# Transposing x unscaled, scaling the forget products by token, and forming the normalised input alongside

## The reference

```python
def rms_norm(x, gain):
    y = x * lax.rsqrt(jnp.mean(x * x, axis=-1, keepdims=True) + NORM_EPS)
    return y * gain

h = rms_norm(x, pre_norm)
z = einsum('btd,dn->btn', h, w_in)          # 12848 columns, split by use:
(a_q, a_kc, a_vc, a_ks, a_vs, a_kw, a_vw, a_gate, a_silu,
 b_v, b_silu, c_q, c_f, c_i, c_silu, merge_logits) = split(z)

# the gated recurrence ("HGRN2") reads the forget columns c_f first
f = lb + (1 - lb) * sigmoid(c_f)            # per token and channel
logf, k = log(f), 1 - f                     # then cumulative sums of logf by chunk
...                                         # attention, pooling, gates
out = einsum('btd,de->bte', merged, w_out)
x = x + rms_norm(out, post_norm)
```

## Time and profile before

| | us |
|---|---|
| median of 3 runs (lowest, highest) | 480.6 (480.55, 480.81) |
| the profiled execution | 480.7 |
| its span, first to last instruction | 478.8 |

### The profile page before, as it was taken

The page is one execution under the profiler, slowest core; times in us unless marked ns, Lnnn a source line. Parts: engine busy times, 40 slices in busy tenths (PEclk is TensorE's granted clock), DMA queues, the critical chain, the costliest instruction groups (busy, mean ns, idle before and its releaser), DMA issues.

```text
span 478.8 us, 9549 instructions
## 1 busy us (share of the span) xinstructions
PE 471.5 (98%) x3884; PEld 459.6 (96%) x3884; DVE 347.8 (73%) x611; ACT 278.0 (58%) x418; POOL 170.0 (35%) x157
## 2 busy tenths in 40 slices
...
GB/s 296 324 165 182 225 134 130 141 54 175 177 144 122 142 266 210 99 174 179 88 252 104 166 97 89 90 175 89 176 96 169 177 152 192 185 244 241 175 1 90
DMA packets 75994, 76.47 MB, mean 160 GB/s; under 512 B 5745, under 2 KB 74609, under 8 KB 75950
## 3 DMA queue, kind: packets, MB, share of 16 engines
...
q10 hardware_dynamic: 288, 0.18, 0.1%
...
## 4 chain that ended last, share of the span: by engine, by line
PE 88%; DVE 6%; DMA 3%; ACT 2%; issue 1%; SPq 0%; DVEq 0%; ACTq 0%
PE ps L1030 72%; PE ps L1194 3%; DMA W<-w_in 3%; DVE WL L662 2%; PE ps L1052 2%; PE ps L1145 2%; PE ps L1134 1%; PE ps L1161 1%; PE ps L1056 1%; PE ps L1148 1%; PE ps L1071 1%; PE ps L1163 1%; PE ps L1162 1%; PE ps L1099 1%; DVE hL L918 1%
## 5 line engine op out<-in xcount | busy, mean ns | idle before, releaser
L1030 PE MATMUL ps<-hH,WL 128*128 128x256 f32 x688 | 195.7, 288 | 0.6 <-DVE WL L662 0.6
L1030 PE MATMUL ps<-hH,WH 128*128 128x256 f32 x688 | 194.8, 284 | 0.0
L1030 PE MATMUL ps<-hL,WH 128*128 128x256 f32 x688 | 194.8, 284 | 0.0
L662 DVE TENSOR_TENSOR WL<-W,WH 128x2048 fp32r<-128x2048 f32 (+1 forms) x66 | 153.3, 2323 | 17.6 <-PE ps L1030 17.4
L452 ACT ACTIVATE WH<-W 128x2048 fp32r<-128x2048 f32 (+1 forms) x66 | 124.7, 1889 | 37.8 <-PE ps L1030 32.5
L1030 PEld LDWEIGHTS ps<-hH,WL 128*128 128x128 f32 x688 | 130.7, 192 | 2.1 <-DVE WL L662 1.3
L1030 PEld LDWEIGHTS ps<-hL,WH 128*128 128x128 f32 x688 | 131.8, 192 | 0.8 <-issue 0.7
L1030 PEld LDWEIGHTS ps<-hH,WH 128*128 128x128 f32 x688 | 131.8, 192 | 0.0
L414 POOL TENSOR_SCALAR R<-R,st 128x256 f32<-128x256 f32 x32 | 29.2, 923 | 76.8 <-DVE st L841 76.8
L1030 PE MATMUL ps<-bH,WL 128*128 128x256 f32 x192 | 54.9, 286 | 0.0
L1030 PE MATMUL ps<-bH,WH 128*128 128x256 f32 x192 | 54.3, 283 | 0.0
...
## 6 DMA issues: line engine op xcount, KB each, us to landing
...
```

The costliest lines, as they stand in the source:

```text
L662: dve.tensor_tensor(slab_view(WL[:, s % 2], s), slab_view(W[:, s % 3], s), slab_view(WH[:, s % 3], s), ALU.subtract).then_inc(s_lo, 1)
L1030: mm = pe.matmul(o, l, r, start=(at == 0 if mixed else k0 + k == 0 and j == 0), stop=(at == len(order) - 1 if mixed else k0 + k == KC - 1 ...
```

## The change

Rows of x are turned as they come, with no norm. ScalarE and VectorE evict them times the gain into bH and bL, buffers that are otherwise used by the branch products much later, and slabs 0 to 3 use these. Meanwhile ScalarE squares the first 128 rows and VectorE the second; one root, one reciprocal; VectorE writes each token's factor along the whole row of that token in a 128 x 128 tile (FLAT, two of them), TensorE turns both after slab 0, and ScalarE copies the result as RT, every token's factor on every partition.

The forget slabs are now read by VectorE, PSUM times RT to OC (`read`), and then by ScalarE's sigmoid from OC. The normalised input for all later slabs is made on VectorE in steps 1 and 2 of its loop (`NORM_DVE`, four chunks each, to HN), rounded to hH by ScalarE in steps 2 and 3 (`NORM_HI`), and its low part hL made by GpSimd; slab 4 waits for both (`s_nlo`). `forget(p)` goes to step p+2, logarithms to steps 3, 4, 5, 5, scans to 3, 5, 6, 8. Slab 0 is loaded as two quarters and a half, its high parts are made in four pieces, and 8 instead of 18 warm-up products are run. Slab 2 joins slab 1 in doing its WH matmuls first. The identity is loaded alone and only once.

```diff
 NS = len(SLABS)
-FIRST_A, FIRST_B = 4, 5
+FIRST_B = 5
 LAST = NS - 5
...
 BY_ACT = ("f", "hq", "hv", "vs", "vw", "bv", "kc", "vc", "q", "ks", "kw", "silu", "merge", "out")
-BY_DVE = ("ks", "kw", "q", "silu", "branch", "out")
+BY_DVE = ("ks", "kw", "q", "silu", "branch", "out", "f")
 ACT_READS = [sum(x[0] in BY_ACT for x in SLABS[:i + 1]) for i in range(NS)]
...
 U0 = 9
-LN_AT = (1, 4, 4, 4)
-SCAN_AT = (2, 5, 6, 8)
+LN_AT = (3, 4, 5, 5)
+SCAN_AT = (3, 5, 6, 8)
 MUL_AT = (7, 10, 11, 14, 15, 18, 19, 22)
...
 NU = HG * TT
-WARM = 18
+WARM = 8
 
...
+        RT, FLAT = TG[:, 0, 0:T], TG[:, 1, 0:T]
+        HN = R[:, 2, :].rearrange("p (c t) -> p c t", c=KC)
...
             src = slab_source(0)
-            sp.dma_start(W[:, 0, 0:FIRST_A, :], src[:, 0:FIRST_A, :]).then_inc(s_first, 16)
-            sp.dma_start(W[:, 0, FIRST_A:KC, :], src[:, FIRST_A:KC, :]).then_inc(s_land[0], 16)
+            for i in range(2):
+                sp.dma_start(W[:, 0, 2 * i:2 * i + 2, :], src[:, 2 * i:2 * i + 2, :]).then_inc(s_first[i], 16)
+            sp.dma_start(W[:, 0, 4:KC, :], src[:, 4:KC, :]).then_inc(s_land[0], 16)
             load_slab(1)
...
             sp.dma_start(K[:, 0:K_ID], consts[:, 0:K_ID]).then_inc(s_consts, 16)
-            sp.dma_start(K[:, K_CMASK:K_ALL], consts[:, K_CMASK:K_ALL]).then_inc(s_consts, 16)
+            sp.dma_start(K[:, K_ONE:K_ALL], consts[:, K_ONE:K_ALL]).then_inc(s_consts, 16)
             sp.dma_start(causal, consts[:, K_CAUSAL:K_CAUSAL + P]).then_inc(s_consts, 16)
...
 
+            pool.wait_ge(s_hi0a, 3)
             pool.wait_ge(s_hi0b, 1)
...
                                ALU.subtract).then_inc(s_lo0p, 1)
+            for half in range(2):
+                c = slice(4 * half, 4 * half + 4)
+                pool.wait_ge(s_nhi, half + 1)
+                pool.tensor_tensor(hL[:, c, :], HN[:, c, :], hH[:, c, :], ALU.subtract).then_inc(s_nlo, 1)
             for p in range(4):
...
                 else:
-                    pool.wait_ge(s_xn, 3)
                     pool.wait_ge(s_xt, 4)
...
             def mix(s):
+                if s in NORM_HI:
+                    half = NORM_HI.index(s)
+                    act.wait_ge(s_nrm, half + 1)
+                    c = slice(4 * half, 4 * half + 4)
+                    act.activation(hH[:, c, :], HN[:, c, :], ACT.Copy).then_inc(s_nhi, 1)
                 for p in range(4):
...
                 elif kind == "f":
-                    act.activation(OC[:, 2 * n:2 * n + 2, :].rearrange("p c t -> p (c t)"), bank(s),
-                                   ACT.Sigmoid).then_inc(s_read_a, 1)
+                    act.wait_ge(s_read_v, DVE_READS[s])
+                    f = OC[:, 2 * n:2 * n + 2, :]
+                    act.activation(f, f, ACT.Sigmoid).then_inc(s_read_a, 1)
                 elif kind in ("kc", "vc"):
...
                     last.then_inc(s_read_a, 1)
-            act.dma_start(K[:, K_ID:K_CMASK], consts[:, K_ID:K_CMASK]).then_inc(s_small, 16)
+            act.dma_start(ident, consts[:, K_ID:K_ID + P]).then_inc(s_ident, 16)
             act.dma_start(V[:], small).then_inc(s_small, 16)
...
             act.activation(st_q[:, 0:1], st_eps, ACT.Sqrt)
-            for i in range(TT):
-                act.wait_ge(s_x[i], 16)
-                link(act.activation(sq[:, i, :], xin[:, i, :], ACT.Square, accum_out=st_x[:, i:i + 1]))
-                act.activation(st_t[:, i:i + 1], st_x[:, i:i + 1], ACT.Sqrt, scale=1.0 / D,
-                               bias=st_eps).then_inc(s_hx, 1)
-            act.wait_ge(s_first, 16)
-            act.activation(WH[:, 0, 0:FIRST_A, :], W[:, 0, 0:FIRST_A, :], ACT.Copy).then_inc(s_hi0a, 1)
-            act.wait_ge(s_small, 32)
+            act.wait_ge(s_x[0], 16)
+            link(act.activation(sq[:, 0, :], xin[:, 0, :], ACT.Square, accum_out=st_x[:, 0:1]))
+            act.wait_ge(s_first[0], 16)
+            act.activation(WH[:, 0, 0:2, :], W[:, 0, 0:2, :], ACT.Copy).then_inc(s_hi0a, 1)
+            act.wait_ge(s_small, 16)
             for c in range(KC):
+                if c == 2:
+                    act.wait_ge(s_first[1], 16)
+                    act.activation(WH[:, 0, 2:4, :], W[:, 0, 2:4, :], ACT.Copy).then_inc(s_hi0a, 1)
+                if c == 4:
+                    act.wait_ge(s_land[0], 16)
+                    act.activation(WH[:, 0, 4:6, :], W[:, 0, 4:6, :], ACT.Copy).then_inc(s_hi0a, 1)
                 act.wait_ge(s_xt, c // 2 + 1)
-                act.activation(hH[:, c, :], ps[:, 2 + c // 2, 256 * (c % 2):256 * (c % 2) + 256], ACT.Copy,
+                act.activation(bH[:, c, :], ps[:, 2 + c // 2, 256 * (c % 2):256 * (c % 2) + 256], ACT.Copy,
                                scale=V[:, V_PRE + c:V_PRE + c + 1]).then_inc(s_hx, 1)
-            hi(1)
+            act.wait_ge(s_sq1, 1)
+            act.activation(st_t, st_x, ACT.Sqrt, scale=1.0 / D, bias=st_eps).then_inc(s_sqrt, 1)
+            act.wait_ge(s_land[1], 16)
+            act.activation(WH[:, 1, 0:4, :], W[:, 1, 0:4, :], ACT.Copy).then_inc(s_hi1, 1)
+            act.activation(WH[:, 1, 4:KC, :], W[:, 1, 4:KC, :], ACT.Copy).then_inc(s_hi, 1)
+            act.wait_ge(s_rt, 1)
+            act.activation(RT, ps[:, 7, 0:T], ACT.Copy).then_inc(s_rb, 1)
             act.wait_ge(s_lbd, 1)
...
                         op0=ALU.mult, op1=ALU.add).then_inc(s_scan, 1)
-                if 1 <= s <= 4:
-                    forget(s - 1)
+                if s in NORM_DVE:
+                    half = NORM_DVE.index(s)
+                    for c in range(4 * half, 4 * half + 4):
+                        last = dve.scalar_tensor_tensor(
+                            out=HN[:, c, :], in0=ps[:, 2 + c // 2, 256 * (c % 2):256 * (c % 2) + 256],
+                            scalar=V[:, V_PRE + c:V_PRE + c + 1], in1=RT, op0=ALU.mult, op1=ALU.mult)
+                    last.then_inc(s_nrm, 1)
+                if 2 <= s <= 5:
+                    forget(s - 2)
                 for h in range(HG):
...
                 kind, n = SLABS[s][:2]
+                if kind == "f":
+                    dve.wait_ge(s_prod, s + 1)
+                    dve.wait_ge(s_rb, 1)
+                    scale = RT.rearrange("p (a t) -> p a t", a=1).to_broadcast((P, 2, T))
+                    dve.tensor_tensor(OC[:, 2 * n:2 * n + 2, :], bank(s).rearrange("p (c t) -> p c t", c=2), scale,
+                                      ALU.mult).then_inc(s_read_v, 1)
+                    return
                 if kind not in BY_DVE:
...
             dve.memset(CKS[:, :, :, NCMP:16].bitcast(F32), 0.0)
-            for i, n in ((0, D), (1, D // 2), (1, D)):
-                if n == D // 2 or i == 0:
-                    dve.wait_ge(s_hx, i + 1)
-                    link(dve.reciprocal(st_r[:, i:i + 1], st_t[:, i:i + 1]))
-                part = xin[:, i, (D // 2 if i and n == D else 0):n]
-                dve.tensor_scalar(part, part, st_r[:, i:i + 1], None, ALU.mult).then_inc(s_xn, 1)
-            dve.wait_ge(s_hi0a, 1)
-            dve.tensor_tensor(WL[:, 0, 0:FIRST_A, :], W[:, 0, 0:FIRST_A, :], WH[:, 0, 0:FIRST_A, :],
-                              ALU.subtract).then_inc(s_lo0, 1)
-            dve.wait_ge(s_land[0], 16)
-            dve.tensor_copy(WH[:, 0, FIRST_A:KC, :], W[:, 0, FIRST_A:KC, :]).then_inc(s_hi0b, 1)
-            dve.wait_ge(s_small, 32)
+            dve.wait_ge(s_x[1], 16)
+            dve.scalar_tensor_tensor(out=sq[:, 1, :], in0=xin[:, 1, :], scalar=1.0, in1=xin[:, 1, :], op0=ALU.mult,
+                                     op1=ALU.mult, accum_out=st_x[:, 1:2]).then_inc(s_sq1, 1)
+            dve.wait_ge(s_small, 16)
             for c in range(KC):
-                dve.wait_ge(s_hx, TT + 2 * (c // 2) + 2)
-                dve.scalar_tensor_tensor(out=hL[:, c, :], in0=ps[:, 2 + c // 2, 256 * (c % 2):256 * (c % 2) + 256],
-                                         scalar=V[:, V_PRE + c:V_PRE + c + 1], in1=hH[:, c, :],
+                if c in (0, 2):
+                    dve.wait_ge(s_hi0a, c // 2 + 1)
+                    dve.tensor_tensor(WL[:, 0, c:c + 2, :], W[:, 0, c:c + 2, :], WH[:, 0, c:c + 2, :],
+                                      ALU.subtract).then_inc(s_lo0, 1)
+                if c == 4:
+                    dve.wait_ge(s_land[0], 16)
+                    dve.tensor_copy(WH[:, 0, 6:KC, :], W[:, 0, 6:KC, :]).then_inc(s_hi0b, 1)
+                dve.wait_ge(s_hx, 2 * (c // 2) + 2)
+                dve.scalar_tensor_tensor(out=bL[:, c, :], in0=ps[:, 2 + c // 2, 256 * (c % 2):256 * (c % 2) + 256],
+                                         scalar=V[:, V_PRE + c:V_PRE + c + 1], in1=bH[:, c, :],
                                          op0=ALU.mult, op1=ALU.subtract).then_inc(s_lx, 1)
-            dve.wait_ge(s_hi0b, 1)
-            dve.tensor_tensor(WL[:, 0, FIRST_A:FIRST_B, :], W[:, 0, FIRST_A:FIRST_B, :], WH[:, 0, FIRST_A:FIRST_B, :],
+            dve.tensor_tensor(WL[:, 0, 4:FIRST_B, :], W[:, 0, 4:FIRST_B, :], WH[:, 0, 4:FIRST_B, :],
```

(51 more changed lines are left out.)

10 lines of the change are left out of this document (7 added, 3 removed).

## The result

The changed kernel takes 493.4 us (median of 4 runs, 492.8 to 494.3) against 480.6, a ratio of 1.0266 with an interval of 1.0254 to 1.0279: 12.8 us slower. The forecast was 492.2 us, 11.6 slower. The profiled execution took 493.5 us, its span is 491.5.

A forecast was written before the change was run, and what follows sets the result against it. VectorE sets the pace before 39.55 us, TensorE after it. The early start is lost in the queue, slab 10 starts 11.5 us late: 480.7 + 11.5 = 492.2 us, forecast case 488.5 to 496.5 (chance 0.66).

The forecast's parts named there:

- The head: Start up to slab 1: first product near 7.9, slab 0 ending near 13.8, TensorE 1.7 us earlier, VectorE not earlier.
- The queue: VectorE's loop with ScalarE and GpSimd, step by step: scan(0) at 36.8, lo(9) at 68.7 instead of 57.20, 11.5 us lost.
- The places of the loss: Slab 4 waits for GpSimd's second low half, TensorE idle 5.4 us; later chains make slab 10 11.5 us late.
- The faster case: VectorE's queue in steps 0 to 3 stays ahead of TensorE, so the early start survives: 479 us; chance 0.06.
- The clock: TensorE's clock may fall after idle gaps: mostly hidden, no term; if repeatedly, 497 to 500; chance 0.07 shared with more disturbance.
- The rule on the shared port: VectorE's evictions, with at most one SBUF input, escape GpSimd contention and stay at 0.6; otherwise some 2 us more.

The follow-up runs named there:

- experiment 6: The kernel before, with VectorE evicting the four forget products (times ones) and ScalarE's sigmoid reading them from there: 481.7 us, ratio 1.0020.
- experiment 1: Also called a_hi_both: the changed kernel, with ScalarE making both high halves of the normalised input in step 2: 494.3 us.
- Experiment 2: The edit of experiment 1 on the changed kernel, plus the logarithms of pair 0 in step 2, ahead of sigmoid(2) and hi(5): 491.4 us.
- experiment 3: The edits of Experiment 2, plus exponentials of pair 0 ahead of the logarithms of pair 3, which move to step 6: 488.2 us.
- b_all_three: The kernel before with VectorE's forget evictions, eight extra normalisation-like passes and the moved steps, without new head, high copies or GpSimd's subtractions: 490.1 us.
- experiment 10: Also called b_order_fixed: kernel before with moved forget and scan steps, pair 0's logarithms in step 2, its exponentials ahead of pair 3's logarithms: 483.3 us.
- experiment 12: The kernel b_norm with 12 unused 128x128 products on TensorE ahead of slab 4: 484.3 us.
- a_head_only: The changed kernel's new head alone, with no scaling by token and the loop steps as before the change: 480.6 us, ratio 1.0002.
- b_norm: The kernel before, with eight unused VectorE passes of 128x256 from PSUM in steps 1 and 2: 485.2 us.

## Why the prediction was right, step by step

**The head.** Right in kind: 8.18 and 14.65 for 7.9 and 13.8. The 0.85 us missing at the end of slab 0 are the last low part, made at 13.4 and not at 12.4: VectorE's chunks ended at 12.7, and the pass itself (128x256, beside GpSimd's) took 0.80 for 0.42 before. VectorE's loop began at 19.13, not 18.5: `lo(1)` began at 14.38 (14.05 before), and the small constants waited for an exponential that now stands behind the copy of RT.

**A wait I did not see.** Slab 2 waits 1.28 us, since its bank is free only when sigmoid(0) has run, and that waits for VectorE's eviction and a table load (19.89 to 21.8). It was hidden: slab 4 was later by more. Likewise slab 8 waits 1.65 us for ScalarE's read of slab 6, queued behind the exponentials; `lo(9)` and the masks came later still.

**The queue.** This is the step that carried the sum, and it held: scan(0) 38.1 for 36.8, `lo(5)` done 46.3 for 45.6, slab 6 at 52.7 for 52.0, slab 7 at 60.7 for 59.2, `lo(9)` at 70.1 for 68.7. The 0.6 us of the late loop start and 0.6 of forget(0) explain the 1.3 us of scan(0). Forget(0) took 3.58 us (27.87 to 31.45), not 2.97: I had taken a disturbed forget from the earlier trace rows, where GpSimd's instructions are short; one of 2.4 us holds VectorE's pass for its whole length. Against that, `lo(5)` beside GpSimd took 2.33, not 2.9 (experiment 6), and 0.6 came back. Then scan(1) and what belongs to it took 4.3 us (52.54 to 56.84), not 3.3: its four scans took 3.36 beside GpSimd's last two instructions. With forget(3) a little shorter than assumed, that is how 0.7 us at slab 6 became 1.5 at slab 7 and 1.4 at `lo(9)`.

**The places of the loss.** The text said that slab 4's wait for the second low half loses 5.4 us and that later chains lose more. That slab 4 waits is right (4.47), but experiment 1 shows that this wait is not worth anything by itself: with slab 4 two microseconds earlier the kernel was 0.9 slower. The text's own next steps said as much, since its sum ends at `lo(9)` and not at slab 4. The loss is set by when VectorE reaches forget(3) and ScalarE the exponentials. Experiment 2 moves scan(0) by 2.5 us (38.84 to 36.31) and the end by 2.9; experiment 3 takes forget(3) out of the exponentials' way and moves the end by 3.2.

**How it divides.** In the kernel before: moved steps alone 6.9, passes of the normalisation alone 4.5, evictions alone 1.0, all three 9.4. The new head is 0.0. The rest, 12.8 less 9.4, is 3.4 us for the high copies, GpSimd's subtractions and the later start of VectorE's loop in the changed kernel; that part was not run alone. The two traces say where it lies: scan(0) starts at 38.10 against 34.70 in b_all_three, 3.4 us later. VectorE's loop starts 0.4 us later (19.13 for 18.69), forget(0) takes 2.0 more (3.58 for 1.56), and ScalarE needs 0.9 more from sigmoid(2) to the end of the logarithms, as it has a high copy of 1.04 us in between.

The moved steps' 6.9 us are 4.3 of ScalarE's order, and of the other 2.6 the clock has 1.6 (experiment 10); of the passes' 4.5 the clock has 0.9 (experiment 12).

**The faster case.** Its price was wrong. I gave -1.7 us for the head if VectorE kept up; a_head_only has VectorE's old loop and gains nothing, because VectorE already paced slabs 4 and 5. The profile had said so, and the rival should have been priced at nil.

**The clock.** A term that I held at zero, rightly for this kernel, but not for its neighbours. Stretches of the changed kernel, granted clock after POOL's busy time:

```profile
35.00:37.00 2.00, 0.00 (x0) 0.00 (x0) 0.00 (x0) 1.97 (x3) 1.32 (x1) 1.00 0.76 187
37.00:39.00 2.00, 0.88 (x7) 0.91 (x8) 0.90 (x3) 1.06 (x2) 1.02 (x1) 0.98 0.94 333
39.00:41.00 2.00, 2.00 (x11) 2.00 (x10) 1.97 (x6) 0.00 (x0) 0.41 (x1) 0.50 0.01 4
41.00:43.00 2.00, 2.00 (x14) 2.00 (x13) 1.93 (x3) 0.00 (x0) 2.00 (x3) 0.67 0.00 0
```

It was at 0.50, half of 2.4 GHz, from 39 to 41 after TensorE had been idle from 33.6 to 38.1, and slab 4 took 38.12 to 45.6, 7.5 us where slab 5 took 6.0 (46.38 to 52.40). `lo(5)` came at 46.3, so nothing was lost, as foreseen. The waits of 2.06 and 1.65 us ahead of slabs 7 and 8 left the clock at 1.00, while in b_order_fixed it fell at 52.2, right after a wait of 1.91. In b_norm the fall followed an idle stretch from 33.5 to 36.8 and cost 0.9 us, since `lo(5)` was ready before the slow slab ended. It fell in eight of the twelve kernels of the experiments, in b_order_fixed at a cost as well (experiment 10). In the other six a later slab still waited for a low part or for ScalarE, so that the differences of experiments 1 to 3 are not the clock's: in a_hi_both slab 5 took 8.7 us, but slab 7 started at 61.44, just when `lo(7)` was done. (The prediction read 0.60 in the earlier trace rows as half a microsecond at the lower level; 0.60 is the mean of 0.2 at 1.00 and 0.8 at 0.50. Nothing hangs on it.)

**The rule on the shared port.** All evictions took 0.68 us, also the one at 43.39 in the middle of GpSimd's differences; b_norm's eight passes took 468 to 476 ns, four of them beside GpSimd. The Trainium skill (SBUF — State Buffer, Who interferes with whom) says that an instruction with one SBUF input and outside the two-port modes does not contend, and that where there is contention one side is blocked for the other's whole instruction. The trace agrees on both: 0.68 beside GpSimd's work, and in a_hi_both 4.84 for two short passes beside 4.82 of subtractions. The forget passes read one SBUF tile as well (OC, with st for a scalar), so by that rule they contend only if they run in a two-port mode; which mode they run in is not shown here.
